# Seven products of block sums in place of eight for seven eighths of the second mixer's projection

## The reference, cut to what matters

```python
hp = rmsnorm(xp, norm_mix[1]); hs = rmsnorm(xs, norm_mix[1])
proj = h @ w_in                       # w_in: 1024 x (512 q | 512 k | 1024 v | 1024 o | 16 gates)
q, k = proj[..., :512], proj[..., 512:1024]
v, o = proj[..., 1024:2048], proj[..., 2048:3072]
i_pre, log_f = gates[..., :8] + b_i, log_sigmoid(gates[..., 8:] + b_f)
hh, C, n, m = mlstm_chunkwise(q, k, v, i_pre, log_f, c0, n0, m0)
out = (sigmoid(o) * (rmsnorm_per_head(hh) * head_norm)) @ w_out
x = x + out                           # then x = x + hier_moe(rmsnorm(x)), and a last rmsnorm
```

## Time and profile before

| | us |
|---|---|
| median of three runs | 1360.45 (1357.02 to 1362.40) |
| profiled execution, its own time | 1364.08 |
| its span | 1362.1 |
| TensorE busy in it | 1204.9 (88%) |
| VectorE, ScalarE, POOL busy | 404.4, 253.9, 250.2 |
| projection of the second mixer, from the end of the experts' load issues to its last row | 701.5 to 928.7 |

### The profile page before, as it was taken

How to read it: one execution, slowest core, us unless ns; L and a number is a source line. 1 busy time by engine, 2 the same in 40 slices (tenths; PEclk the granted TensorE clock), 3 DMA queues, 4 the chain that set the end, 5 groups by cost and what they waited for, 6 DMA issues and landing times.

```text
span 1362.1 us, 16370 instructions
## 1 busy us (share of the span) xinstructions
PE 1204.9 (88%) x6249; PEld 633.4 (47%) x6249; DVE 404.4 (30%) x856; ACT 253.9 (19%) x600; POOL 250.2 (18%) x284
## 2 busy tenths in 40 slices
PE   7999999998899899778878999998899899877880
PEld 6755675566545433233325754445744533333330
DVE  6742116644303521111126201113611612111115
ACT  2111117733203010000013100014412101000001
POOL 2351404322000111111010000304810011111102
PEclk8999999999899899888989999998999899889995
DMA  8321308599876599999956140402357689999966
GB/s 297 105 70 71 132 2 287 185 341 366 309 309 262 200 412 420 421 420 420 412 203 204 63 128 0 139 0 87 109 167 316 243 325 420 420 420 420 419 250 216
DMA packets 104511, 340.25 MB, mean 250 GB/s; under 512 B 22478, under 2 KB 40850, under 8 KB 80618
## 3 DMA queue, kind: packets, MB, share of 16 engines
q1 hardware_dynamic: 89800, 303.24, 58.5%
q0 software_dynamic: 14336, 35.80, 7.3%
q10 hardware_dynamic: 290, 0.08, 0.0%
HBM read 322.45 MB, written 31.31 MB: 260 GB/s over the span
## 4 chain that ended last, share of the span: by engine, by line
PE 58%; SPq 14%; DMA 12%; DVE 7%; POOL 3%; issue 2%; ACT 1%; PEldq 1%; PEld 0%; POOLq 0%; DVEq 0%; ACTq 0%
SPq L1355 10%; PE ps L1565 9%; PE ps L2071 8%; DMA moe_gu<-in_moe_w_up 7%; PE ps L613 6%; PE ps L1490 6%; PE ps L2022 4%; SPq L1377 4%; PE ps L1583 4%; PE ps L609 4%; DMA fox_arena<-negs_rows 3%; PE ps L957 2%; PE ps L969 2%; PE ps L980 2%; DMA moe_gu<-expert_rows 1%
## 5 line engine op out<-in xcount | busy, mean ns | idle before, releaser
L1565 PE MATMUL ps<-moe_gu,rows 128*64 128x512 f32 x1024 | 245.5, 635 | 55.6 <-DMA moe_gu<-in_moe_w_up 52.3
L1565 PEld LDWEIGHTS ps<-moe_gu,rows 128*64 128x64 f32 x1024 | 81.0, 146 | 199.8 <-issue 192.3
L1852 DVE TENSOR_TENSOR turned<-turned,ps 128x256 f32<-128x256 f32 x32 | 13.5, 421 | 305.1 <-ACT turned L1668 305.1
L1449 POOL DMA_INDIRECT expert_rows<-turned,moe_row x32 | 32.1, 1002 | 392.0 <-ACT turned L1678 359.9
L1583 PE MATMUL ps<-moe_wd,moe_rowsel 128*64 128x512 f32 x352 | 80.4, 598 | 1.9 <-DVE turned L1857 1.9
L1668 ACT ACTIVATE turned<-ps 128x256 f32<-128x256 f32 x32 | 12.3, 384 | 302.8 <-PE ps L1565 302.8
L2071 PE MATMUL ps<-mwblk,turned 128*128 128x512 f32 x128 | 56.0, 594 | 1.5 <-DVE vaug L2290 1.5
L448 POOL TENSOR_TENSOR fox_arena<-fox_arena 128x512 f32<-128x512 f32 x32 | 44.6, 1416 | 64.9 <-PE ps L609 55.2
L2071 PE MATMUL ps<-m_arena,turned 128*128 128x512 f32 x128 | 55.7, 593 | 0.7 <-ACT m_arena L2175 0.7
L613 PE MATMUL ps<-x,fox_arena 128*128 128x288 f32 x224 | 56.0, 406 | 0.0
L2022 PE MATMUL ps<-turned,mwblk 128*128 128x288 f32 x224 | 54.6, 406 | 0.0
(11 more groups left out here) (386 smaller groups left out, 1735.0 us busy)
## 6 DMA issues: line engine op xcount, KB each, us to landing
moe_gu<-in_moe_w_gate SPq DMA_DIRECT2D x56, 1024.0 KB, 21.8
moe_gu<-in_moe_w_up SPq DMA_DIRECT2D x56, 1024.0 KB, 24.1
moe_wd<-in_moe_w_down SPq DMA_DIRECT2D x44, 1024.0 KB, 24.1
rows<-in_moe_w_down SPq DMA_DIRECT2D x20, 1024.0 KB, 22.6
fox_arena<-in_cache_v POOLq DMA_DIRECT2D x32, 512.0 KB, 12.6
fox_arena<-in_fox_w_in SPq DMA_DIRECT2D x6, 2048.0 KB, 10.1
fox_arena<-in_cache_k SPq DMA_DIRECT2D x20, 512.0 KB, 9.9
moe_gu<-in_moe_w_gate SPq DMA_DIRECT2D x16, 512.0 KB, 10.1
```

The source lines that it names most:

```text
L1565: mm = pe.matmul(ps[h, 2 + p % 2, :].rearrange("s (k f) -> s k f", k=2), xT[:, c, h], gu[s][:, half, :, c, :], start=(c == 0), stop=(c == ...
```

## The change

`mlstm_project` is rewritten. Of the keys the first two groups are left as they were; the other two groups, all four of the queries (three units of two groups), the values (pair 0) and `o` (pair 1) are computed with tokens, features and columns each split in two: seven products of block sums (`factors`) in place of eight. A unit's product is 4 matmuls of 288 columns, a pair's is 2 tiles of 4 matmuls of 512 columns.

- VectorE makes four sums of activations, S1 to S4, over `x` (`spent`), and so needs `x` stored first: SyncE stores each tile to a new `x_rows` once it is combined, ahead of the load of block 1; VectorE waits for all five stores before S1. The next phase, `mlstm_cells`, loads `x` back after its gate rows, and the last layer's adds wait for it.
- POOL makes the sums of weights: four sums of 128x512 for each of three units, and four of 4 pieces of 128x512 for each pair. They go over `vaug`, `Cs`, slot 0 and the weights themselves.
- ScalarE keeps three of a unit's (pair's) partial results and VectorE adds the others to them.
- The order of the tiles becomes 0, 1, L, 2, 3 (`ORDER`); the loads of `expert_rows`, issued by the phase before, keep theirs.
- The sample rows of values and `o` are computed in strips of 32 (`sample_rows`), ahead of pair 0 and inside pair 1.
- The loads of `state_C` move behind pair 0, and block 5's load goes behind the sixth product of pair 0.

```diff
-SET = 56
+SET = 58
+        x_dram = nc.dram_tensor("x_rows", (TOK, D), F32, kind="Internal").ap()
...
-                if layer == 0:
-                    dve.wait_ge(x_again, 16 * NT)
+                dve.wait_ge(x_again, 16 * NT * (layer + 1))
...
+            ORDER = (0, 1, L, 2, 3)
+            def factors(B, T1, T2, T4):
+                return [(A[0][0], B[0][0]), (S1, T1), (S2, T2), (S4, B[1][1]), (S3, B[0][1]), (A[0][1], B[1][0]), (A[1][1], T4)]
...
-                sp.wait_ge(combined, 2 * NT)
+                for at, n in enumerate(ORDER):
+                    sp.wait_ge(combined, 2 * (at + 1))
+                    sp.dma_start(x_dram[n * P:n * P + ROWS[n], :], x[0:ROWS[n], n, :]).then_inc(x_out, 16)
                 load_block(sp, 1)
...
-                sp.wait_ge(v_done, 2 * L + 1)
+                sp.wait_ge(w_product, 12)
+                sp.wait_ge(tw_ready, 4)
                 load_block(sp, 5)
...
             def pool_(pool):
...
+                pool.wait_ge(combined, 2 * NT)
+                for unit in range(UNITS):
+                    pool.wait_ge(w_in[min(unit, 1)], 16)
+                    first_sums(pool, ch, narrow_blocks(unit), *T_narrow[unit][0:2])
+                    last_sum(pool, ch, narrow_blocks(unit), *T_narrow[unit][1:3])
+                    third_sum(pool, ch, narrow_blocks(unit))
+                    pool.sem_inc(t_ready, 1)
+                for pair in range(2):
+                    B, (T1, T2) = wide_blocks(pair), T_wide[pair]
+                    if pair:
+                        pool.wait_ge(w_product, 14)
+                        pool.wait_ge(w_in[1], 32)
+                        pool.wait_ge(w_in[2], 32)
+                    else:
+                        pool.wait_ge(w_in[2], 16)
+                        pool.wait_ge(w_in[0], 32)
+                    first_sums(pool, ch, B, T1, T2, tw_ready)
+                    pool.wait_ge(sv_done[pair], 1)
+                    third_sum(pool, ch, B)
+                    pool.sem_inc(tw_ready, 1)
+                    pool.wait_ge(w_product, 14 * pair + 4)
+                    last_sum(pool, ch, B, T2, T1)
+                    pool.sem_inc(tw_ready, 1)
...
+            BANKS = ((0, 4, 5), (1, 4, 5), (0, 4, 5))
+            def unit_product(pe, unit, k):
...
+                if k == 1:
+                    pe.wait_ge(t_ready, unit + 1)
...
+                if k == 6:
+                    pe.wait_ge(summed, 3 * unit + 2)
...
             def pe_(pe):
...
+                narrow(pe, 1, 0, 2, k_done)
+                for unit in range(UNITS):
...
+                    for k in range(7):
+                        unit_product(pe, unit, k)
                 pe.wait_ge(bent, 1)
-                wide(pe, 2, v_done, v_kept)
-                pe.wait_ge(v_kept, 2 * NT)
-                wide(pe, 4, o_done, o_kept)
+                sample_rows(pe, 0)
...
+                for k in range(7):
+                    wide_product(pe, 0, k)
...
+                turn_gates(pe)
+                for k in range(7):
+                    wide_product(pe, 1, k)
+                    if k == 1:
+                        sample_rows(pe, 1)
+                    if k == 2:
+                        sample_scores(pe)
...
+                dve.wait_ge(x_out, 16 * NT)
+                ch(dve.tensor_tensor(S1, A[1][0], A[1][1], ALU.add))
...
+                unit_sums(0)
...
+                for n in range(NT):
+                    sp.dma_start(x[0:ROWS[n], n, :], x_dram[n * P:n * P + ROWS[n], :]).then_inc(x_again, 16)
```

More of the change, by code:

```diff
@@ L2012, in pool_, with pieces, first_sums, last_sum @@
                         mask_gate_rows(pool, tri01[:, p], k, masked)
-            def pool_root(pool, n):
-                pool.wait_ge(meaned, n + 1)
+            def pieces(block):
+                return [slice(0, KH)] if block.shape[2] == P else [slice(c, c + 1) for c in range(KH)]
+            def first_sums(eng, ch, B, T1, T2, after_each=None):
+                for out, left, right in ((T1, B[0][1], B[0][0]), (T2, B[1][1], T1)):
+                    for c in pieces(out):
+                        ch.step(eng.tensor_tensor(out[:, c], left[:, c], right[:, c], ALU.subtract))
+                    ch.wait()
+                    if after_each is not None:
+                        eng.sem_inc(after_each, 1)
+            def last_sum(eng, ch, B, T2, T4):
+                for c in pieces(T4):
+                    ch.step(eng.tensor_tensor(T4[:, c], B[1][0][:, c], T2[:, c], ALU.subtract))
+                ch.wait()
+            def third_sum(eng, ch, B):
+                for c in pieces(B[0][1]):
+                    ch.step(eng.tensor_tensor(B[0][1][:, c], B[1][1][:, c], B[0][1][:, c], ALU.subtract))
+                ch.wait()
+            def pool_root(pool, at):
+                n = ORDER[at]
+                pool.wait_ge(meaned, at + 1)
                 pool.tensor_tensor(rstd[:, n:n + 1], ms[:, n:n + 1], const("minus_half")[:, 0:1], ALU.pow).then_inc(rooted, 1)
@@ new lines, in mlstm_project @@
+            BANKS = ((0, 4, 5), (1, 4, 5), (0, 4, 5))
+            def unit_product(pe, unit, k):
+                x_bank, y_bank, z_bank = BANKS[unit]
+                bank = (x_bank, y_bank, x_bank, y_bank, x_bank, z_bank, x_bank)[k]
+                if k == 0 and unit == 2:
+                    pe.wait_ge(copied, 4)
+                if k == 1:
+                    pe.wait_ge(t_ready, unit + 1)
+                    if unit:
+                        pe.wait_ge(summed, 3 * unit - 2)
+                    else:
+                        pe.wait_ge(s_ready, 1)
+                        pe.wait_ge(k_kept, 1)
+                if k in (2, 3, 4):
+                    pe.wait_ge(copied, 4 * unit + k - 1)
+                if k == 5 and unit:
+                    pe.wait_ge(summed, 3 * unit)
+                if k == 6:
+                    pe.wait_ge(summed, 3 * unit + 2)
+                T1, T2, T4 = T_narrow[unit]
+                a, b = factors(narrow_blocks(unit), T1, T2, T4)[k]
+                for c in range(KH):
+                    mm = pe.matmul(ps[:, bank, 0:HT], b[:, c, :], a[:, c, :], start=(k in (0, 1, 5) and c == 0), stop=(c == KH - 1),
+                                   skip_group_check=True)
+                mm.then_inc(product, 1)
@@ new lines, in sample_rows @@
+            def sample_rows(pe, pair):
+                for m in range(2):
+                    pe.wait_ge(w_in[(2 + 2 * pair + m) % 3], 16 * ((2 + 2 * pair + m) // 3 + 1))
+                if pair:
+                    pe.wait_ge(w_summed, 6)
+                for c in range(KC):
+                    for m in range(2):
+                        for u in range(2):
+                            at = m * SAMP + u * HS
+                            mm = pe.matmul(ps[at:at + HS, (4 if pair else 6) + m, :], halves[:, c, u, HP:HT],
+                                           wblk[(2 + 2 * pair + m) % 3][:, c, :], start=(c == 0), stop=(c == KC - 1))
+                mm.then_inc(sv_done[pair], 1)
@@ L2123, in pe_ @@
                 idle_products(pe, 7, 5)
-                for n in range(3):
+                for n in ORDER[0:3]:
                     flip(pe, n)
@@ new lines, in narrow_places, with narrow_scale, wide_place @@
+            def narrow_places(unit, u, m):
+                out, g = (kT, 2 + m) if unit == 0 else (qT, 2 * (unit - 1) + m)
+                return [(out[:, g, u * HP:(u + 1) * HP], slice(0, HP)),
+                        (out[:, g, PROMPT + u * HS:PROMPT + (u + 1) * HS], slice(HP, HT))]
+            def narrow_scale(unit):
+                return MK ** -0.5 if unit else 1.0
+            def wide_place(pair, u, m, j):
+                if pair:
+                    return og[:, 2 * u + j, m * 512:m * 512 + 512]
+                return vaug[:, 2 * u + j, m * 4:m * 4 + 4, 0:MV]
@@ L2187, in act_ @@
[L2187 to L2192 removed]
+                for j in range(2):
+                    act.wait_ge(w_product, 12 + j + 1)
+                    act.activation(wide_place(0, 1, 0, j), wide_bank(0, j), ACT.Copy).then_inc(w_copied, 1)
@@ L2308, in dve_ @@
+                wide_sum(1, 2)
+                for k, (hf, mb) in enumerate(((0, 1), (1, 1), (0, 0), (1, 0))):
+                    for j in range(2):
+                        dve.wait_ge(o_opened, 2 * k + j + 1)
+                        open_gate(hf, mb, j)
                 ch.wait()
```

320 lines of the change are left out of this document (201 added, 119 removed).

## The result

| | before | after |
|---|---|---|
| median of 15 runs each, same chip, us | 1361.89 (1355.03 to 1367.59) | 1353.71 (1349.44 to 1358.16) |
| ratio, 95% interval | | 0.9948 (0.9927 to 0.9969) |
| profiled execution, its own time | 1364.08 | 1357.84 |
| its span | 1362.1 | 1356.2 |

The change makes the kernel 0.5% faster by the ratio: 7 us, with an interval of 4 to 10; the medians differ by 8.2. The forecast was 13.4 us and 1347.0; the time lies 0.7 us above 1353, the upper end of the range.

The account below looks back on a forecast made before the run. TensorE's products were taken to bound the projection from 737.8 on, a load and VectorE's adds its head. -22.4 + 5 + 2 + 1.5 + 0.5 = -13.4 us took the median from 1360.45 to 1347.0, range 1340.5 to 1353.

Parts of the forecast that it names:

- What TensorE is spared: In the projection: fewer key, query, value and `o` products, two copy waits gone, a shorter end; together 22.4 us less.
- both waits for copies: In the projection, `wide` for the values (0.7 us) and `o` (1.5 us) would no longer wait for copies.
- The price of the gate products: In the projection, pair 1's first product would pay the 1.7 us that the sample rows paid behind the gate products.
- The head: At the projection's start: 5 us for VectorE's wait for the late sample tile, 2 us for TensorE's lower clock.
- POOL and VectorE: In unit 0 of the projection, TensorE waits 1.5 us before the seventh product, between 0 and 10.3.
- After the projection: Ahead of the cells' gate-row loads, ten more semaphore clears cost 0.5 us; reloading `x` costs 0, up to 5.6.
- VectorE and POOL shut each other out, or the reload delays the gate rows: Rival on projection and cells: the 1.5 us becomes 6 to 8, or 4 come on top; 1352, chance 0.14.
- The head costs little: Rival: TensorE's list absorbs the late tile and the clock stays up; 5 and 2 shrink to 2; 1342, chance 0.17.
- The gain stays within what can be told: Rival: a 2.19 us wait for VectorE's additions in three units and two pairs, 11 us; 1356.5, chance 0.06.
- TensorE waits for sums of weights: Rival: half of POOL's 44 sums stand bare before products, 28 us, decided at pair 1; 1375, chance 0.04.
- The signs I had named: Wrong if `narrow` begins within 2 us of 737.8, products wait for POOL, or phases after 928.7 change over 2 us.
- the forecast's first part: The projection's saving on TensorE's products, waits and end: 22.4 us.

Follow-up runs that it names:

- the two delayed kernels: The kernel before with 25, and with 10, semaphores cleared a second time ahead of the cells' gate-row loads: cells 83.37 and 83.89 us.
- the two helped kernels: Kernel before with cells' clears on VectorE and two idle products: 1357.22 us; changed kernel with these, sample rows third, unit 1's sums delayed, `x` reloaded last: 1334.64.

## Why the prediction was wrong

Means over all profiles in which the stage in question is as in the kernel named (before: head, projection and rest from five profiles, cells from two; after: head from six, projection from six, cells from four, rest from nine):

| stage | before | after | difference | forecast |
|---|---|---|---|---|
| head | 33.7 | 38.9 | +5.2 | +7 |
| projection | 190.6 | 171.4 | -19.2 | -22.4 + 1.5 = -20.9 |
| cells | 81.3 | 84.9 | +3.6 | +0.5 |
| rest | 353.3 | 353.1 | -0.2 | 0 |
| sum | | | -10.6 | -13.4 |

**What TensorE is spared: right.** Where POOL is kept off the chain, the projection takes 169.5 to 169.9 us, 21 less than before. The sample strips cost what the strips of 64 did (7.00 for 64 instructions of two blocks, 7.04 for 32 before), and both waits for copies went. The price of the gate products moved to pair 1 in seven of nine profiles; in the two of the changed kernel as it is, nobody paid it (7.13 us behind them), so their projections look 1.7 us better than the forecast had reason to expect.

**The head: right in kind, 2 us too dear.** The add started at 719.26 behind a wait of 5.66 (forecast 718 and 6), the clock fell as feared. I had 5 for the lateness and 2 for the clock; together they cost 5.2, and the reordered load gives all of it back and some more. What each of the two cost, no run separates.

**POOL and VectorE: right, and slightly undersized.** TensorE's wait was 2.0 us on average instead of 1.5, and it is gone in the kernel that separates them. What I left out is what follows the wait: in four of six profiles the clock fell behind it and cost 1.7 us on top. Averaged over the six that is 1.1 us, which with the 0.5 makes up the 1.7 us missing from this stage.

**After the projection: the step that failed.** It had two terms, +0.5 for the clears and 0 for the reload of `x`, and it took for granted that the cells would otherwise be as long as before. Measured: +3.6. The clears were right, 0.54 to 0.56 us. The reload was not free: 0.3 to 0.4. Of the shift of about 1.4 us at the last wait (62.45 to 63.8 or 63.9) some 0.5 is in neither. Most of it, 0.4 us, lies at one place: VectorE's third adding of a state, which starts 39.45 us into the stage before and 40.96 after.

```profile
968.18 0.69 DVE L2748 TENSOR_TENSOR Cs<-Cs,ps 128x512 f32<-128x512 f32 x1 [0.21 <-DVE mhb L2722]
...
956.99 0.69 DVE L2977 TENSOR_TENSOR Cs<-Cs,ps 128x512 f32<-128x512 f32 x1 [0.59 <-DVE mhb L2951]
```

It waits 0.59 us in all six changed kernels that clear on SyncE, and 0.21 in all others. What it waits for there stays open. And 2.2 us are the clock: the profile that I read showed 3.01 us of waiting at 991 with the clock at 1.00 behind it, and I took that for a property of the stage. It was the one profile of eleven in which that wait went unpunished. So the step that failed is "the cells as long as before": +3.6 us came where +0.5 was counted. The mean of before in this table rests on two profiles, one without and one with a late fall; with the two delayed kernels taken in (less their delay) it would be 82.0 rather than 81.3, and the loss 2.9, of which 1.5 are the clock.

**The rest of the gap is not settled.** The stages sum to -10.6 us, and the medians say -8.2 with an interval of -4 to -10. The stage table does not cover what lies ahead of the head, whose length varied between 698 and 710 us over the profiles of both kernels. Its mean is 702.3 us in the five of before and 705.1 in the nine of changed kernels. The 2.8 us between them would fill the gap, but they lie within that scatter, so they show nothing.

**The rivals.** "VectorE and POOL shut each other out, or the reload delays the gate rows" gave 1352, 1.7 us from the result. Both of its mechanisms were real, but small (2.0 and 0.4 us); its number came about by the clock. "The head costs little" is out by the 38.9 us. "The gain stays within what can be told" is out as told: VectorE's additions held TensorE up once, in unit 0, and not in five places. "TensorE waits for sums of weights" did not happen: pair 1 shows no wait for POOL. The signs I had named worked as alarms: `narrow` began 7.4 us later than 737.8 (2.0 of them because the head itself began later), no wait for POOL, and "if the phases after 928.7 change their length by more than 2 us" was the one that went off.

**What the change is worth.** By the comparison of the two helped kernels, 21 to 23 us. In their two profiles the projection differs by 21.5 us (190.98 and 169.47), near the 22.4 of the forecast's first part, and the head and the cells by 1.9 and 1.5. As delivered, the change loses some 14 of them: 5 to the load order, 2 to POOL beside the chain and 1 to the clock behind that, 3.6 to the cells; the rest is not accounted for.

## What to carry to other kernels

When a change reorders who is consumed when, reorder the loads with it: one line in the phase before was worth 6.5 us of head here (38.9 to 32.4) and 5.9 us of the time by the ratios, nearly as much as the change itself gave. Look at what stands between the start of a phase and its first load on the issuing queue: 58 clears of 55 ns were 3.2 us of critical path, and VectorE had room for them. In the kernel before the same move, together with the idle products, ended the last wait only 0.5 us earlier, so look also at what comes next on the path. And a wait of TensorE like those of 2 and 3 us here should be priced with the slow products that can follow it, even if the profile at hand shows none; two idle products in the 3 us wait kept the clock up in all three kernels that had them.

## What the runs showed of the hardware

- A single wait of 3.0 us ahead of small products cost anything between 0 and 3.25 us afterwards, by the clock's falling at once, 1 to 2 us later, or not. The granted clock behind it in the first profile of after, stretches of 4 us:

```profile
976.00:980.00 4.00, 1.00 (x10) 0.81 (x8) 2.58 (x8) 0.05 (x1) 1.15 (x1) 0.90 0.94 329
980.00:984.00 4.00, 4.00 (x25) 3.45 (x26) 2.13 (x8) 1.49 (x10) 0.00 (x0) 0.50 0.60 184
984.00:988.00 4.00, 4.00 (x14) 2.75 (x14) 0.69 (x1) 2.04 (x9) 2.65 (x3) 0.74 0.68 212
```

- The clock also fell where TensorE never stood still: behind 2.9 us of small products, mostly of 8 columns, between two wide ones (0.67 in the stretch from 856 of the kernel with POOL kept apart), with 1.7 us lost in the products right behind them. It did so in 11 of 14 profiles.
- Transfers issued behind others can delay them: the gate rows of 128 and 256 KB landed 8.6 and 7.6 us after their issue (middle of two loads each) with the reload of `x` behind them, 7.9 and 7.3 with the reload moved away, and 7.8 and 7.2 in the kernel before.
- Ten more `sem_clear` on SyncE cost 0.54 us, 54 ns each.
